# Gated attention's first three decay levels: from masked 128x128 products to small block products copied by ScalarE, with three level buffers

## The reference

```python
def step(state, inp):
    qc, kc, vc, gc = [t.astype(jnp.float32) for t in inp]
    b = jnp.cumsum(gc, axis=1)
    o_inter = jnp.einsum('bihk,bhkv->bihv', qc * jnp.exp(b), state)
    diff = b[:, :, None] - b[:, None]
    decay = jnp.exp(jnp.where(mask, diff, -jnp.inf))
    attn = jnp.einsum('bijhk,bjhk->bijh', qc[:, :, None] * decay, kc)
    o_intra = jnp.einsum('bijh,bjhv->bihv', attn, vc)
    ...
```

## Time and profile before

| | us |
|---|---|
| median of 3 runs | 2143.74 (2143.57 to 2145.15) |
| profiled execution, its own time | 2146.2 |
| profiled execution, span | 2144.1 |
| TensorE busy (matmuls) | 2114.8 |
| VectorE busy | 1216.0 |
| ScalarE busy | 730.8 |
| TensorE's mean granted clock | 0.998 |

### The profile page before, as it was taken

How to read it: one execution, slowest core, us unless ns; L and a number is a source line. 1 busy time by engine, 2 the same in 40 slices (tenths; PEclk the granted TensorE clock), 3 DMA queues, 4 the chain that set the end, 5 groups by cost and what they waited for, 6 DMA issues and landing times.

```text
span 2144.1 us, 27795 instructions
## 1 busy us (share of the span) xinstructions
PE 2114.8 (99%) x10063; PEld 1727.4 (81%) x10063; DVE 1216.0 (57%) x1931; ACT 730.8 (34%) x1020; POOL 88.4 (4%) x124
## 2 busy tenths in 40 slices
PE   8999999999999999999999999999999999999998
PEld 7888888888888777888888888888866678888887
DVE  7434446587677886435446544434678645445344
ACT  4222223433336443222224222222467742222223
POOL 0000000000000000000000000000025400000000
PEclk9999999999999999999999999999999999999999
DMA  6333433222153424445454333332310123333321
GB/s 170 98 98 98 104 90 98 83 81 62 44 146 94 94 70 106 114 107 113 104 111 115 88 101 95 98 98 81 106 40 2 40 59 97 100 89 98 99 85 61
DMA packets 357980, 195.02 MB, mean 91 GB/s; under 512 B 14891, under 2 KB 349878, under 8 KB 357894
## 3 DMA queue, kind: packets, MB, share of 16 engines
q1 hardware_dynamic: 355270, 184.21, 30.3%
q0 software_dynamic: 2624, 9.67, 2.8%
HBM read 191.07 MB, written 2.79 MB: 90 GB/s over the span
## 4 chain that ended last, share of the span: by engine, by line
PE 72%; DVE 6%; issue 1%; ACT 1%; DVEq 0%; POOL 0%; ACTq 0%
PE ps L1539 19%; PE ps L1541 19%; PE ps L1540 19%; PE ps L2071 2%; PE ps L1723 1%; PE ps L2059 1%; PE ps L2040 1%; DVE w_lo L841 1%; DVE index_scores L1394 1%; PE ps L1738 1%; PE ps L1740 1%; PE ps L1739 1%; DVE stat L1392 1%; PE ps L1558 1%; PE ps L1560 1%
## 5 line engine op out<-in xcount | busy, mean ns | idle before, releaser
L484 ACT ACTIVATE w_hi<-w_raw 128x1024 fp32r<-128x1024 f32 x351 | 371.7, 1060 | 1042.2 <-PE ps L1541 969.1
L1539 PE MATMUL ps<-h_hi,w_hi 128*128 128x512 f32 x1552 | 605.5, 390 | 0.0
L1541 PE MATMUL ps<-h_hi,w_lo 128*128 128x512 f32 x1552 | 603.9, 389 | 0.0
L1540 PE MATMUL ps<-h_lo,w_hi 128*128 128x512 f32 x1552 | 603.9, 389 | 0.0
L841 DVE TENSOR_TENSOR w_lo<-w_raw,w_hi 128x1024 fp32r<-128x1024 f32 x351 | 428.7, 1222 | 286.5 <-ACT w_hi L484 286.2
L1539 PEld LDWEIGHTS ps<-h_hi,w_hi 128*128 128x128 f32 x1552 | 291.3, 188 | 61.9 <-issue 1.7
L1540 PEld LDWEIGHTS ps<-h_lo,w_hi 128*128 128x128 f32 x1552 | 291.3, 188 | 60.4
L1541 PEld LDWEIGHTS ps<-h_hi,w_lo 128*128 128x128 f32 x1552 | 291.3, 188 | 60.3
L1539 PE MATMUL ps<-act_hi,w_hi 128*128 128x512 f32 x704 | 274.0, 389 | 0.0
L1541 PE MATMUL ps<-act_hi,w_lo 128*128 128x512 f32 x704 | 273.9, 389 | 0.0
L1540 PE MATMUL ps<-act_lo,w_hi 128*128 128x512 f32 x704 | 273.9, 389 | 0.0
(11 more groups left out here) (325 smaller groups left out, 2240.9 us busy)
## 6 DMA issues: line engine op xcount, KB each, us to landing
w_raw<-in_ffn_w_gate SPq DMA_DIRECT2D x88, 512.0 KB, 3.8
w_raw<-in_ffn_w_up SPq DMA_DIRECT2D x88, 512.0 KB, 3.8
w_raw<-in_ffn_w_down SPq DMA_DIRECT2D x64, 512.0 KB, 3.9
w_raw<-in_hy_w_in SPq DMA_DIRECT2D x44, 512.0 KB, 3.8
w_raw<-in_ffn_w_down SPq DMA_DIRECT2D x32, 384.0 KB, 3.4
w_raw<-in_hy_w_out SPq DMA_DIRECT2D x16, 512.0 KB, 4.1
acum_rows<-acum_scratch POOLq DMA_DIRECT2D x4, 1024.0 KB, 10.3
bias_rows<-line_scratch POOLq DMA_DIRECT2D x8, 512.0 KB, 6.7
```

The source lines that it names most:

```text
L484: act.activation(w_hi[:, s, :], w_raw[:, s, :], ACT.Copy).then_inc(hi_ready, 1)
L1539: pe.matmul(ps[:, bank, :], wh, rh[:, k, :], start=k == 0, stop=False)
L1540: pe.matmul(ps[:, bank, :], wh, rl[:, k, :], start=False, stop=False)
L1541: mm = pe.matmul(ps[:, bank, :], wl, rh[:, k, :], start=False, stop=k == nk - 1)
```

## The change

LEVELS stays 7, and BLOCKED = 3 says how many levels are made as blocks.

Matmuls. For levels 0, 1 and 2 `level(l)` no longer multiplies 128 by 128. For each chunk, head and block it multiplies the s older positions with the s newer ones, so that there are 16 matmuls of 64 columns by 64, 32 of 32 by 32 and 64 of 16 by 16. They are written to the partitions of the block's older positions, starting at 2s times the block's number, side by side for the four heads.

Copies. ScalarE's new `blocks_out(l)` brings them to their place in `gla_attn`, one copy for each block and all chunks and heads: 64x1024 numbers, two times 32x512, four times 16x256. VectorE's `masked(0)` to `masked(2)` are gone, and `masked(3)` waits for all seven copies (`g_blk`).

Buffers. Three level buffers take turns, the third in `gla_gate`, which isn't needed for the gate before these steps end. `diff(l)` waits from l = 3 on, for level l-3.

Order. ScalarE's step s is now: `level_exp(s+1)`, the `gla_v` copies where s is 3 or 7, `blocks_out(s-1)` for s = 1 to 3, `produce_hi`. VectorE's is: `diff(s+1)`, (`mult(0)` in step 0), `produce_lo`, `mult(s)`, and `masked(s-1)` from s = 4 on.

```diff
-LEVELS = 7
+LEVELS, BLOCKED = 7, 3
...
+        gla_levels = [gla_level[:, 0, :, :], gla_level[:, 1, :, :], gla_gate[:, 0:GH, :]]
...
                 def level_exp(l):
                     act.wait_ge(g_diff, 2 * (l + 1))
-                    act.activation(gla_level[:, l % 2, :, :], gla_level[:, l % 2, :, :], ACT.Exp, scale=1.0 / GTAU).then_inc(g_exp, 1)
+                    act.activation(gla_levels[l % 3], gla_levels[l % 3], ACT.Exp, scale=1.0 / GTAU).then_inc(g_exp, 1)
+
+                def blocks_out(l):
+                    s = P >> (l + 1)
+                    act.wait_ge(g_zero, 1)
+                    act.wait_ge(g_lvl, TT * (l + 1))
+                    for b in range(1 << l):
+                        k0 = 2 * s * b
+                        act.activation(gla_attn[k0:k0 + s, :, :, k0 + s:k0 + 2 * s],
+                                       ps[k0:k0 + s, 0:TT, 0:GH * s].rearrange("p c (h t) -> p c h t", h=GH), ACT.Copy).then_inc(g_blk, 1)
...
                 for s in range(8):
+                    if s + 1 < LEVELS:
+                        level_exp(s + 1)
                     if s % 4 == 3:
...
+                    if 0 < s <= BLOCKED:
+                        blocks_out(s - 1)
                     produce_hi(n + 9 + s + SLOTS)
-                    if 0 < s < LEVELS:
-                        level_exp(s)
...
-                    if l >= 2:
-                        dve.wait_ge(g_lvl, TT * (l - 1))
+                    if l >= 3:
+                        dve.wait_ge(g_lvl, TT * (l - 2))
...
                 def masked(l):
                     for c in range(TT):
                         dve.wait_ge(g_lvl, TT * l + c + 1)
-                        if l:
-                            dve.wait_ge(g_mask, TT * (l - 1) + c + 1)
+                        if l == BLOCKED:
+                            dve.wait_ge(g_blk, (1 << BLOCKED) - 1)
+                        else:
+                            dve.wait_ge(g_mask, TT * (l - 1 - BLOCKED) + c + 1)
...
-                mult(0)
                 for s in range(8):
-                    if 0 < s < LEVELS:
-                        diff(s)
+                    if s + 1 < LEVELS:
+                        diff(s + 1)
+                    if s == 0:
+                        mult(0)
                     produce_lo(n + 9 + s + SLOTS)
                     if 0 < s < LEVELS:
                         mult(s)
-                    if s:
+                    if s > BLOCKED:
                         masked(s - 1)
...
+                    if l <= BLOCKED:
+                        pe.wait_ge(g_blk, (1 << l) - 1) if l else None
                     for c in range(TT):
-                        if l:
-                            pe.wait_ge(g_mask, TT * (l - 1) + c + 1)
+                        if l < BLOCKED:
+                            s = P >> (l + 1)
+                            for h in range(GH):
+                                for b in range(1 << l):
+                                    k0 = 2 * s * b
+                                    older, newer = (gla_levels[l % 3][:, h, c * P + t0:c * P + t0 + s] for t0 in (k0, k0 + s))
+                                    mm = pe.matmul(ps[k0:k0 + s, c, h * s:(h + 1) * s], older, newer, start=True, stop=True, skip_group_check=True)
+                            mm.then_inc(g_lvl, 1)
+                            continue
+                        if l > BLOCKED:
+                            pe.wait_ge(g_mask, TT * (l - 1 - BLOCKED) + c + 1)
```

## The result

The changed kernel takes 2152.06 us (median of 7 runs, 2151.09 to 2154.0) against 2143.57 before (7 runs, 2143.15 to 2145.24): a ratio of 1.004, 95% interval 1.003 to 1.005. It is slower by 8.5 us where 8.4 were forecast. The profiled execution has a span of 2150.4 and a time of its own of 2152.19.

A forecast was written before the change was run, and what follows sets the result against it. TensorE was taken to bound the kernel before, a ScalarE-VectorE lock step the changed stretch. The order's +7.6 us (+7.5 before dropped hundredths) and +0.8 for the clock gave +8.4: 2152.1 us, range 2149.8 to 2156.0.

The forecast's parts named there:

- Order: ScalarE and VectorE: lo waits behind diff(s+1), exp(s+1), copies and hi, mult behind lo; 8.79 us per loop plus copies.
- The sum of +7.5 us: Start of level 5 on TensorE: 495.5 us in place of 488.0, from the new order of the other engines.
- One sign: TensorE before level 3: an idle time waiting for mult, with level 3 starting near 474.9 us.
- Small products: TensorE, levels 1 and 2: 0.03 us a record, bounds 0.014 and 0.067, giving levels of 1.9 and 3.8 us.
- the level's length cancelled: TensorE: level 1 may last to 456.5 and level 2 to 468.8 us before ScalarE would wait for them.
- rival D: Not slower: hi and lo still run ahead of exp, TensorE stays the bound and saves 2.3 us, 2141.4; chance 0.04.
- A wait that the prediction had only in passing: Step 3, ScalarE: four gla_v copies add 2.40 us to the loop ahead of lo(3).
- Clock: TensorE: idle times of about 2 us may bring stretches at 1.2 GHz; one after level 5 counts in full, 1.7 us.
- The term of +0.8: TensorE's clock: half of one 1.7 us stretch at 1.2 GHz added to the total, bounds 0 and 1.7.
- B: TensorE: small matmuls cost 0.06 us or more each whatever their columns, +9.7, up to +12 with clock; chance 0.20.
- C: ScalarE and VectorE: the loop is shorter than added up, total +1 to +7 us; chance 0.07.

The follow-up runs named there:

- run 1: The changed kernel with ScalarE's hi (high half of a weight unit) moved ahead of exp(s+1) and the block copies: 2137.60 us, ratio 0.9967.
- run 2: The kernel before with the new order and three level buffers only, all levels 128x128 with masked copies, no block copies: 2155.55 us, ratio 1.0051.
- run 4: The changed kernel with the block copies moved behind hi, exp(s+1) still ahead of hi: 2148.11 us, ratio 1.0018.
- run 5: The kernel of run 1 with each small product of levels 0, 1 and 2 made twice: 2145.09 us, ratio 1.0004.
- run 9: The kernel of run 6 with diff and exp one step early and hi ahead of exp: 2136.08 us, ratio 0.9965.
- run 3: The changed kernel with diff, exp and hi in the order of before, block copies following exp: 2137.59 us, ratio 0.9971.
- run 6: The kernel of run 3 with levels 3 to 6 and the diagonal also made from 32x32 blocks: 2139.48 us, ratio 0.9982.
- run 7: The kernel of run 1 with level 2 making each of its small products four times: 2149.13 us, one run.

## Why the prediction was right, step by step

**Order: right, with its mechanism.** The times of lo, forecast and measured: 448.84 and 449.01, 458.73 and 458.94, 471.28 and 471.64, 480.07 and 480.34, 491.31 and 491.47. Level 5 was forecast for 495.5 and came at 495.74, 0.37 of which is this trace's later start. Level 3 was forecast for 474.86 and came at 475.46. The sum of +7.5 us stands against 7.44 in the stretch. Runs 1, 2 and 4 show the cause: with hi in front the loss is gone, with the order alone it is all there, and the copies' place makes 3.7 us of it in the traces (4.0 in the medians). One sign failed: level 3 was to start after an idle TensorE, and its row has no idle time before it.

**Small products: mis-sized, and it didn't show.** The prediction took 0.03 us a record for 32 and 16 columns with bounds of 0.014 and 0.067. Measured are 0.016 and 0.009: level 2 lasts 463.62 - 462.49 = 1.13 us, not 3.8 plus a switch. (It ran at 1.2 GHz here; in run 1, at 2.4 GHz, it is no shorter: 1.21 from its start to the next unit's.) The lower bound was above the second value, and going by columns from the earlier trace rows (0.028 and 0.014) would have been too high for both. The number of columns doesn't tell these two apart. Level 1 writes 32 columns a record, to partitions from 0 and from 64 in turn, at 0.016, and as much when the burst is twice as long (run 5). Level 4 of run 9 writes 32 columns too, but to partitions from 0, 32, 64 and 96 in turn:

```profile
472.31 1.35 PE L1753 MATMUL ps<-gla_level 128*32 128x32 f32 x128
473.59 0.50 PE L1769 MATMUL ps<-w_hi,h_hi 128*128 128x512 f32 x1
```

These are 1.28 us for 128 records, 0.010 each, next to the 0.009 of level 2, with 16 columns to the same four places. Level 0 writes all its records to one place, at 0.058. TensorE saves 5.8 us, not 2.3: from the start of level 0 to that of level 3 it takes 27.08 us before (442.88 to 469.96) and 21.26 in run 1. Since the other engines set the pace, the level's length cancelled, as the prediction says; but rival D's time was wrong by this term: with TensorE as the bound it is 2137.6, not 2141.4. The rule of the Trainium skill that the prediction cites ("TensorE: Matmul & The Clock Gate", Part 1), a start every 25 ns at the least, doesn't hold for these products either, which go to changing starting partitions: 9 ns. The Trainium skill ("TensorE: Matmul & The Clock Gate", Part 3), on products in several tiles of the array, gives about 4 ns between starts; the trace lies between the two.

**A wait that the prediction had only in passing.** The projection unit of step 3 waits 3.69 us for ScalarE's first `gla_v` copy, which stands behind exp. The prediction had level 2 last almost until that copy. It cost little in the end: the unit was through at 475.46, where mult's second half had ended at 473.92 + 1.22 = 475.14, so level 3 started 0.3 us late and without an idle time, and level 5 depends on lo and the masked copies, which this doesn't touch.

**Clock: right that it falls, wrong where it counts.** The windows after, columns as in the earlier trace rows:

```profile
455.60:462.46 6.86, 3.83 (x17) 2.82 (x16) 3.52 (x4) 3.25 (x4) 0.00 (x0) 1.00 0.13 30
462.46:472.70 10.24, 6.52 (x140) 5.36 (x141) 3.30 (x3) 6.75 (x10) 0.00 (x0) 0.50 0.12 35
472.70:500.00 27.30, 25.48 (x160) 22.36 (x159) 21.45 (x24) 6.78 (x5) 0.00 (x0) 1.00 0.22 60
```

It fell to 1.2 GHz once, for 10.24 us, from the start of level 2, behind its 3.06 us of idle time, until 472.70, and not after level 5. The projection unit at half speed ended at 475.46, 0.3 us after mult: that is its whole cost. The term of +0.8 has no place in this trace. The median difference is nevertheless 8.5 and the stretch's 7.4, so the timed runs held about a microsecond that the profiled one doesn't show. The profiled pair differs by 6.3 only in its spans (2150.4 and 2144.1), since the trace before has another 3.41 us at 1.2 GHz, at 1724.87, and the one after hasn't; across it the offset falls by 1.55. The execution profiled before is also 2.6 us above its median (2146.2 against 2143.57), the one after is at its own. Such a stretch elsewhere, 1.7 us each, is of the size of the spread between runs. Which runs have one wasn't profiled, and so the last microsecond stays open; that the sum hit the median to 0.1 us is partly luck.

**The rivals.** B (small products at 0.06 or more) falls by the 0.009 measured; C (a shorter loop) falls by the times of lo; D (hi not behind exp) isn't what the program does, though run 1 shows what it is worth.

## What to carry to other kernels

An instruction moved ahead on an in-order engine brings its wait with it, and all that stands behind it waits too: before moving one, list what is queued behind it and who waits for that. An earlier start for an engine's operands pays only where that engine sets the pace (0 us in run 3, some 3 us between runs 6 and 9). A burst of 128 records of small products was cheap here (1.2 us) with a projection unit on either side; 256 in a row cost a gap of 2.4 us, which long work between the two halves removed.

## What the runs showed of the hardware that was not expected

- The price of a small fp32 product depends on how many places its outputs go to in turn: 0.016 us a record for 32 columns to two starting partitions (0 and 64), 0.010 for 32 columns to four (0, 32, 64, 96). With 16 columns to the same four it is 0.009, hardly less; with 64 columns to one it is 0.058. The 9 ns are the same at 1.2 GHz (128 records in 1.26 us of busy time at 463.59 in run 7) as at 2.4 GHz (1.22 at 459.59).
- Many such records in a row stop between groups of 128, for 2.4 to 2.8 us where the supply is behind (the first stop in run 7 is 0.48), until 2.3 to 2.4 us after a 16 KB packet of the instruction queue; over 512 records the mean is 0.021 us. The first gap comes after 135 to 167 of them in runs 5 and 7; in runs 6 and 9, where level 3 follows level 2's burst by one projection unit, one of 0.7 came after 110, 2.6 to 2.7 us after such a packet. The changed kernel's own 128 records of level 2 had none.
- A masked copy of 32 partitions takes longer than one of 128 with the same 512 elements a row: four in 3.03 us against 2.57.
